# An RWKV, attention, expert and mixer block on one core: group norm beside the gate products, modulation sums in the recurrence

## What is computed

```python
h = rmsnorm(x, norm1_g);  p = h @ w_in
y_a = rwkv7_bidirectional(p_rwkv, ...) @ w_o_rwkv      # ends in a group norm and a gate:
#   y = (y - mean) * rsqrt(var + GN_EPS) * lnx_g + lnx_b     mean and var over each head's 64 channels
#   y = (y + bonus * v) * (sigmoid(gl) @ g_up)
y_b = neighbourhood_attention_2d(q, k, v, ...) @ w_o_na
g_a, g_b = split(sigmoid(gate_logits + b_gate))
x = x + (g_a * y_a + g_b * y_b) @ w_out
x = x + hierarchical_moe(rmsnorm(x, norm2_g), ...)     # 32 experts, 2 per token
# second block: modulation from one row c and one row c_ctx
silu_c @ w_mod + b_mod        # 1024 x 6144, six vectors of 1024
silu_cc @ w_mod + b_mod       # the first two of them for the context
# then the mixer (Hyena, GLA, GatedDeltaNet), the MLP, the final norm
```

## Time and profile before

| | |
|---|---|
| median of 3 runs | 2638.59 us (2636.98 to 2642.66) |
| the profiled execution | 2632.08 us |
| its span | 2630.2 us |
| PE busy | 2106.9 us, 80% |
| DVE busy | 1116.4 us, 42% |
| mean granted clock of TensorE | 0.864 of 2.4 GHz |
| RWKV core | 281 to 706.3 us |
| group norm and gate | 706.3 to 737.0 us |
| output block | 737.0 to 937.8 us |
| modulation, norm | 937.8 to 965.0, 965.0 to 981.8 us |
| router, dispatch | 981.8 to 1010.0, 1010.0 to 1039.0 us |

### The profile page before, as it was taken

How to read it: one execution, slowest core, us unless ns; L and a number is a source line. 1 busy time by engine, 2 the same in 40 slices (tenths; PEclk the granted TensorE clock), 3 DMA queues, 4 the chain that set the end, 5 groups by cost and what they waited for, 6 DMA issues and landing times. The chain is left out here.

```text
span 2630.2 us, 38274 instructions
## 1 busy us (share of the span) xinstructions
PE 2106.9 (80%) x16072; PEld 1599.2 (61%) x16072; DVE 1116.4 (42%) x1705; ACT 642.1 (24%) x1131; POOL 439.3 (17%) x518
## 2 busy tenths in 40 slices
PE   5888589999779964766771999877778875899998
PEld 4666378878667764222220787634677775688886
DVE  6544444344476622000004675232355556432333
ACT  4344222322123210111112453200211112331331
POOL 1000164554101102000001000000234330010100
PEclk9999588888789965898895999978788887999999
DMA  4211000000067401898884112300000002233331
GB/s 177 74 59 49 15 2 2 2 2 2 14 224 267 165 19 42 312 354 313 316 326 146 65 62 72 114 15 20 1 2 2 2 2 74 74 103 96 96 96 56
DMA packets 72449, 252.23 MB, mean 96 GB/s; under 512 B 11462, under 2 KB 12902, under 8 KB 71520
## 3 DMA queue, kind: packets, MB, share of 16 engines
q1 hardware_dynamic: 59584, 213.12, 23.6%
q10 hardware_dynamic: 6912, 25.17, 2.6%
q0 software_dynamic: 5792, 11.62, 1.2%
HBM read 243.84 MB, written 14.69 MB: 98 GB/s over the span
## 5 line engine op out<-in xcount | busy, mean ns | idle before, releaser
L208 PE MATMUL ps<-h_hi,weights_hi 128*128 128x512 f32 x728 | 301.3, 414 | 27.0 <-DVE h_lo L619 7.3
L209 PE MATMUL ps<-h_lo,weights_hi 128*128 128x512 f32 x728 | 291.2, 400 | 0.0
L210 PE MATMUL ps<-h_hi,weights_lo 128*128 128x512 f32 x728 | 290.6, 399 | 0.0
L191 DVE TENSOR_TENSOR weights_lo<-ring,weights_hi 128x1024 fp32r<-128x1024 f32 x162 | 198.9, 1229 | 194.1 <-ACT weights_hi L187 194.1
L187 ACT CAST weights_hi<-ring 128x1024 fp32r<-128x1024 f32 x162 | 169.4, 1047 | 351.5 <-PE ps L210 337.4
L1776 PE MATMUL ps<-ring,sp_rowsT 128*64 128x512 f32 x512 | 143.5, 687 | 81.2 <-DMA ring<-stream_in 80.3
L709 POOL TENSOR_TENSOR gdn_M<-xT,const 64x256 f32<-64x256 f32 x144 | 108.3, 752 | 564.3 <-DVE xT L3036 437.2
L208 PEld LDWEIGHTS ps<-h_hi,weights_hi 128*128 128x128 f32 x728 | 141.1, 194 | 74.3 <-issue 18.4
L210 PEld LDWEIGHTS ps<-h_hi,weights_lo 128*128 128x128 f32 x728 | 141.3, 194 | 30.9
L209 PEld LDWEIGHTS ps<-h_lo,weights_hi 128*128 128x128 f32 x728 | 142.0, 195 | 29.3 <-issue 1.9
L1776 PEld LDWEIGHTS ps<-ring,sp_rowsT 128*64 128x64 f32 x512 | 38.9, 150 | 180.3 <-issue 134.4
(11 more groups left out here) (531 smaller groups left out, 3860.9 us busy)
## 6 DMA issues: line engine op xcount, KB each, us to landing
ring<-stream_in SPq DMA_DIRECT2D x354, 512.0 KB, 4.6
w_mod_ring<-w_mod_in ACTq DMA_DIRECT2D x48, 512.0 KB, 5.2
sp_picks<-picks SPq DMA_DIRECT2D x4, 1024.0 KB, 5.0
na_rel<-rel_in POOLq DMA_DIRECT2D x4, 640.0 KB, 6.1
xT<-xT_in SPq DMA_DIRECT2D x4, 512.0 KB, 5.8
xT<-xT_in SPq DMA_DIRECT2D x1, 2048.0 KB, 9.5
h_tok<-h_by_token SPq DMA_DIRECT2D x4, 512.0 KB
x_mid<-xT SPq DMA_DIRECT2D x1, 2048.0 KB, 7.9
```

The source lines that it names most:

```text
L191: eng.tensor_tensor(self.lo[:, i % self.n, :], self.unit(i)[0], self.hi[:, i % self.n, :], ALU.subtract).then_inc(self.k.used, 1)
L208: pe.matmul(out, left[0], right[0], start=start, stop=False, **kw)
L209: pe.matmul(out, left[0], right[1], start=False, stop=False, **kw)
L210: return pe.matmul(out, left[1], right[0], start=False, stop=stop, **kw)
```

## The change

1. The group norm and gate leave their own stage. Their DVE chain is cut in ten steps, one behind each gate unit's `rest` in the output block; the gate products follow gate unit 0 on PE, the transposes gate unit 10. Gate units now use four PSUM banks, not eight, and weights three buffers, not two. The splits of y and of the mix move from POOL to DVE, and are spread over gate units 11 and 13 and over the `w_o` units.
2. The modulation sums leave the output block for the core: seven behind the levels of each step (1, 2, 1, 1, 2), 64 in all, each with a load of its own (64 where there were 48), through two slots of the stream's ring, into a third slot, from which each of the eight sums is written to DRAM. For this the heads' stream stops three units early.
3. `stage_mod` goes. The eight sums are read back (4096 KB) in the router; 32 of the 64 column sums follow the router's logits on PE, 32 the transposes of the dispatch; `mod` and `gain` are formed at the end of the dispatch's DVE list.
4. The norm before the experts is computed at the end of the output block.
5. h, the mix and Hyena's H share two tiles; others are placed over tiles that are free. These change addresses, not operations.

```diff
+MOD_AT = [[7 * t + (0, 1, 3, 4, 5, 7)[lv] for lv in range(6)] for t in range(10)]
+MOD_AT = [[min(n, (MG + 2) * 8) for n in at] for at in MOD_AT]
...
+                def mod_sum(n):
+                    m, b = divmod(n, DB)
+                    dve.wait_ge(mod_in[n % 2].sem, mod_in[n % 2].at(16 * (n // 2 + 1)))
+                    c = k.silu_c[:, b, m // MG:m // MG + 1]
+                    if b == 0:
+                        if m:
+                            dve.wait_ge(mod_saved.sem, mod_saved.at(16 * m))
+                        dve.tensor_scalar(part, wm[n % 2], c, None, ALU.mult).then_inc(mod_done.sem, mod_done.up())
+                    else:
+                        dve.wait_ge(mod_done.sem, mod_done.at(n))
+                        dve.scalar_tensor_tensor(part, wm[n % 2], c, part, ALU.mult, ALU.add).then_inc(mod_done.sem, mod_done.up())
...
                             if t + 1 < N:
                                 bias(t + 1)
+                        for n in range(MOD_AT[t][lv - 1], MOD_AT[t][lv]):
+                            mod_sum(n)
+
+            @block.sync
+            def _(sp):
+                for n in range((MG + 2) * DB):
+                    m, b = divmod(n, DB)
+                    if n >= 2:
+                        sp.wait_ge(mod_done.sem, mod_done.at(n - 1))
+                    sp.dma_start(wm[n % 2], k.dram["w_mod"][m % MG * DB + b]).then_inc(mod_in[n % 2].sem, mod_in[n % 2].up(16))
+                    if b == 1 and m:
+                        save(sp, m - 1)
...
+                    if i == 0:
+                        pe.wait_ge(got.sem, got.at(48))
+                        for t in range(NT):
+                            mm = pe.matmul(k.ps[:, 4 + t, :], lora[:, 2, t * P:(t + 1) * P], g_up, start=True, stop=True)
+                        mm.then_inc(u_ready.sem, u_ready.up())
+                    if i == 10:
+                        pe.wait_ge(y_done.sem, y_done.at(NT))
...
                 for i in range(16):
-                    w.rest(dve, i + 1)
-                    for u in (2 * i, 2 * i + 1):
-                        mod_sum(dve, mod_seq, u, mod_part[:, u // DB, :], 0)
+                    w.rest(dve, i + 2)
+                    group_norm(i)
...
+                norm.sum(pe)
+                norm.spread(pe)
...
+def mod_sums(k, pe, mod_part, first, last):
+    for m in range(first, last):
+        mm = pe.matmul(k.ps[:, 7, m:m + 1], mod_part[:, m // DB, m % DB * P:(m % DB + 1) * P], k.c("ones")[:, 0:1], start=True, stop=True)
+    return mm
...
+                sp.dma_start(mod_part[:, :, :], k.dram["mod_acc"]).then_inc(part_in.sem, part_in.up(16))
...
+                pe.wait_ge(part_in.sem, part_in.at(16))
+                mod_sums(k, pe, mod_part, 0, 32)
```

More of the change, by code:

```diff
@@ L140, in col, with stream @@
         return self.cols[p0:p1, a + i:a + i + 1]
-    def stream(self, sp, units):
-        end = min(self.taken_at_stage + units + RING, N_UNITS)
+    def stream(self, sp, units, ahead=RING):
+        end = min(self.taken_at_stage + units + ahead, N_UNITS)
         while self.issued < end:
@@ L809, in stage_core @@
         inv = Inverse(k, st, "rw", 0)
+        wm, part = [k.ring[:, (k.issued + i) % RING, :] for i in range(2)], k.ring[:, (k.issued + 2) % RING, :]
+        assert k.issued + 3 == k.taken + RING
         with k.block() as block:
@@ L1370, in stage_merge @@
[L1370 to L1372 removed]
+            rounded, rested, h_scaled = k.sig("rounded"), k.sig("rested"), k.sig("h_scaled")
             @block.tensor
@@ L1418, in _ @@
                 for i in range(16):
-                    w.round(act, i + 1)
-                    load(2 * i)
-                    load(2 * i + 1)
+                    w.round(act, i + 2)
                     w.wait(act, i)
-                    act.activation(g[:, i, :], k.ps[:, i % 8, :], ACT.Sigmoid, bias=k.col("b_gate", i)).then_inc(g_done.sem, g_done.up())
-                for b in range(DB):
-                    act.copy(yab[0][:, b, :], (yaT if b < 4 else ybT)[:, b % 4, :]).then_inc(y_rounded.sem, y_rounded.up())
@@ L1427, in _ @@
-                for i in range(8):
-                    load(32 + 2 * i)
-                    load(33 + 2 * i)
-                    w.round(act, 17 + i)
-                w.wait(act, 23)
-                for i in range(8):
-                    act.wait_ge(m_done.sem, m_done.at(i + 1))
-                    act.copy(mix[0][:, i, :], g[:, i, :]).then_inc(rounded.sem, rounded.up())
-                for i in range(25, 32):
-                    w.round(act, i)
-            def mod_sum(eng, done, u, part, which):
-                eng.wait_ge(mod_in[u % MB].sem, mod_in[u % MB].at(16 * (u // MB + 1)))
-                c = k.silu_c[:, u % DB, which:which + 1]
-                if u % DB == 0:
-                    eng.tensor_scalar(part, wm[:, u % MB, :], c, None, ALU.mult).then_inc(done.sem, done.up())
-                else:
-                    eng.wait_ge(done.sem, done.at(u))
-                    eng.scalar_tensor_tensor(part, wm[:, u % MB, :], c, part, ALU.mult, ALU.add).then_inc(done.sem, done.up())
@@ L1449, in _ @@
-            @block.gpsimd
-            def _(pool):
-                for b in range(DB):
-                    pool.wait_ge(y_rounded.sem, y_rounded.at(b + 1))
-                    pool.tensor_tensor(yab[1][:, b, :], (yaT if b < 4 else ybT)[:, b % 4, :], yab[0][:, b, :],
-                                       ALU.subtract).then_inc(y_rested.sem, y_rested.up())
-                for i in range(8):
-                    pool.wait_ge(rounded.sem, rounded.at(i + 1))
-                    pool.tensor_tensor(mix[1][:, i, :], g[:, i, :], mix[0][:, i, :], ALU.subtract).then_inc(rested.sem, rested.up())
+                    act.activation(g[:, i, :], k.ps[:, i % 4, :], ACT.Sigmoid, bias=k.col("b_gate", i)).then_inc(g_done.sem, g_done.up())
```

380 lines of the change are left out of this document (201 added, 179 removed).

## The result

The changed kernel takes 2657.04 us (median of 5 runs, 2652.9 to 2661.1) against 2636.98 for the kernel before: ratio 1.0079, interval 1.0052 to 1.0105. It is slower by 0.8%, where 2623 was forecast, and outside the range of 2594 to 2656. Its profiled execution took 2654.48 us with a span of 2652.6, so 22.4 more than before.

| stretch | before | after | difference | forecast |
|---|---|---|---|---|
| up to the core | 286.8 | 288.6 | +1.8 | 0 |
| RWKV core | 418.7 | 503.4 | +84.7 | +58 |
| core's end to the router | 276.3 | 198.7 | -77.6 | -77.8 |
| router and dispatch | 58.0 | 63.3 | +5.3 | +4.3 |
| experts to the inverse transform | 732.0 | 728.6 | -3.4 | 0 |

The account below looks back on a forecast made before the run. Serial stretches with little work (group norm, modulation, norm, output block) were to go, while PE paces the core: -73.5 us saved, +58 in the core, -15.5 in sum, so 2623 us, range 2594 to 2656.

Parts of the forecast that it names:

- (a): Group norm's own stage, between core and output block: it goes, saving 30.7 us.
- (b): Output block, norm and modulation: 244.8 us become 197.7, saving 47.1 us.
- (c): Column sums and read-back in router and dispatch: router grows 2.7 us, dispatch 1.6; the 4096 KB read-back costs 0.
- (d): Core, two sums ahead of `scale_state`: PE waits 2.6 us, eight times, 20.5 us.
- (e): Core, one sum ahead of `keep_state`, stretched by POOL's product: 1.1 us late, 9 us for eight (2 to 11).
- (f): Core, two sums behind level 2, delaying `update`: 1.0 us, seven times, 7 us (2 to 17).
- (g): Core, sums at levels 3 and 4 and the first step, where DVE waits for PE anyway: 2.5 us (0 to 6).
- (h): Core, partial sums waiting for their write to DRAM before being begun anew: 11 us (5 to 18).
- (i): Core, PE's slower clock from added idle time: 1 us a step, 8 us; from nothing up to 56.
- the clock turns: Rival: new waits in later core levels bring a second 1.2 GHz stretch each step; up to 2671 us; slower overall: 0.23.
- balance: Rival: a core clock term of 18 to 29 us eats the gain, 2633 to 2644 us; chance 0.15.

Follow-up runs that it names:

- x16: The changed kernel with the two wide tiles back at their old addresses: 2647.9 us, ratio 1.0057 to the kernel before.
- x5: The changed kernel with the two sums ahead of `scale_state` moved right behind it from the third step on: 2621.6 us, ratio 0.9954 to the kernel before.
- x7: x3 with the two sums behind `scale_state` moved ahead of it in six steps: 2597.4 us, ratio 0.9855 to the kernel before.
- x9: The changed kernel with the one sum ahead of `keep_state` moved right behind it from the third step on: 2623.7 us, ratio 0.9971 to the kernel before.
- x14: The changed kernel with two partial-sum buffers and, from the third step on, no sums ahead of `keep_state` or `scale_state`: 2589.3 us, ratio 0.9802.
- x2: The changed kernel with two alternating buffers for the partial sum, one unit less loaded ahead: 2636.6 us, ratio 1.0006 to the kernel before.
- x10: x3 with one sum a step cut in two by columns, its first half ahead of `keep_state`: 2615.7 us, ratio 0.9947 to the kernel before.
- x11: x3 with two sums behind level 2 in place of one, one fewer ahead of the decays: 2581.7 us, ratio 0.9812 to the kernel before.
- x6: x3 with one sum a step moved from behind `keep_state` to ahead of it, seven times: 2620.6 us, ratio 0.9938 to the kernel before.
- x3: The changed kernel with the sums moved into DVE's idle gaps and two partial-sum buffers: 2583.9 us, ratio 0.9795 to the kernel before.
- x1: The changed kernel with the same 64 sums moved into DVE's idle gaps, one partial-sum buffer kept: 2594.9 us, ratio 0.9843 to the kernel before.
- x4: The changed kernel with each sum covering 8 of 1024 columns, loads and writes whole: 2597.9 us, ratio 0.985 to the kernel before.
- x12: x8 with seven sums in most steps and only two steps with a third sum behind `scale_state`: 2574.1 us, ratio 0.9794 to the kernel before.
- x8: x3 with eight sums in most steps, three behind `scale_state`, and few at start and end: 2574.3 us, ratio 0.9777 to the kernel before.

## Why the prediction was wrong, step by step

**(a), (b)**, the stages taken out: right. 77.6 us went between the core's end and the router, of 77.8 forecast, and the block with its norm took 197.6, as forecast 197.7. That is partly luck, since the moved tiles made its 384 gate products dearer (an estimate: 6.9 ns each, from the 8.41 and 8.16 us for 36, so 2.7 us); x16, with the old addresses, has 196.1.

**(c)**: router and dispatch grew by 5.3 and not 4.3. The logits waited 1.6 us longer for their small load, beside which the 4096 KB were being read; the read-back itself came in time, 14.1 us behind its issue. My reason for taking it at nothing was weak: the faster row (`x_mid`, 7.9 us for 2048 KB) is a write to DRAM and not a read.

**(d)**, two sums ahead of `scale_state`: forecast 20.5 us of wait; x5 gave 19.6 back, x7 made 13.5 in six steps. That this wait costs no clock is right by itself (x7), but not in the change, where x5 gave back 9.3 us more: there it lies in a long stretch of 17 to 20 us, where x5 has 14. The second stretch isn't what lengthens it: x9, whose second stretches are gone or 3 to 7 us long, still has 17 to 20, and 8.2 us more busy time than x14, where the waits for `scale_state` are gone too (and the saves, which cost no clock in x2). Why the same wait is free in x7 stays open.

**(e)**, one sum ahead of `keep_state`: the wait was right. PE waited 7.0 us more there (11.2 against 4.2) where I had 9: 1.1 to 1.4 us each, as forecast, but in six steps and not eight, since in the last two POOL's product doesn't meet the sum. In all six the sum took 2.3 us and ended 1.08 us behind POOL's product, and five of x10's half sums ended 0.55 us behind it; the rule of the Trainium skill (SBUF — State Buffer, section SBUF: two separate sides), by which the two operations exclude each other for a whole instruction, agrees with that.

**(f), (g)**: 3.8 us in x11 for 7; the waits ahead of the scores grew from 8.6 to 12.0 us in the change, 3.4 for 2.5. **(h)**, the saves: x2 gave back 10.7 us, for 11.

All waits together: idle time +46.2 us where the steps (d) to (h) had 50.

**(i), the clock, is the step that failed.** I took 8 us, "because the largest new wait, (d), lies within the half-clock stretch, and the others are of a microsecond, as those the row already holds". It was 38.5. The reason was wrong in its second half. PE in one step of the kernel before:

```profile
527.43 1.11 PE L941 MATMUL ps<-rw_Ms,rw_kr 64*128 64x64 f32 x16 [0.52 <-DVE rw_state L1129]
...
537.93 0.66 PE L862 MATMUL ps<-const,rw_bk 128*128 128x128 f32 x4 [1.51 <-DVE rw_bk L1089]
```

The step held a wait of 0.52 us ahead of the outputs, some 7 us behind the clock's rise, and the one of 1.51 us later. The change made the first of them 1.6 to 2.0 in six steps, and that is what opens a second half-clock stretch, of 10 us, in five of them: alone, x6 costs 50 us of half clock, x9 gives back 21.6 us of busy time. So the rival "the clock turns" came true, with its sign and its mechanism. It was priced at up to 7 us a step, and from 3.6 on it decides; in the mean over eight steps it was 4.8, and so the result lies between "balance" and 2671.

The clock is what turned the sign: 30.5 us above its term, against a forecast of 15.5 faster. It alone would have given 2653.5, just inside the range. That the result lies outside is the sum of small things: the waits 3.8 us less, and 11.2 more outside the core, of which 7.1 are the recurrence stage's.

The Trainium skill's rule (TensorE: Matmul & The Clock Gate, section HAM oscillation) holds here only in part: not every late level started slow. The save waits (x2), the waits for `scale_state` (x7) and those behind level 2 (x11) left the clock alone: half clock 274 us without the save waits and 271 with them, PE's busy time 376.5 us in x7 and 377.2 in x3, half clock 152 in x11 and 180 in x3.

**Point 5**, the moved addresses at nothing: wrong. The traces show 5.9 us, 4.4 from the head norm on and 1.5 in the output block; by the medians of x16 and the change it is 9.

The recurrence stage's +7.1 us is not the change's: x2, which differs from the change in the core's buffers alone, has 411.7. Its length lies near one of two values in these profiles: 411.5 to 413.5 in the kernel before, x1, x2, x4, x11 and x12, and 418.5 to 419.3 in the other twelve. The granted clock in it is 0.84 before and in x2, 0.82 in the change and in x8.

## What to carry to other kernels

Work put on an engine that is "half idle" is priced by the place, not by the sum: 64 operations in the gaps in which DVE waited for PE cost 5 us of core (x8, with a second buffer for the partial sum), and the same 64 spread behind the levels with one buffer cost 85. Where PE runs in bursts and the clock has just risen, look at the first long wait behind the rise, and let nothing lengthen it; here a microsecond of it cost two to three more in the slower clock (21.9 us for 12.2 in x6, 21.6 for 7.0 in x9). When tiles are moved, compare the interval between products that read them.

## What the runs showed of the hardware that I had not expected

- In the change, x2, x5, x6, x10 and x16 PE waited 1.45 to 2.9 us ahead of the outputs 36 times, mostly from 6 to 8 us behind the clock's rise. 34 times the clock fell within 3 us of the wait's end, for 10 to 14 us (twice for 7). Both exceptions, 1.78 us in the change and 1.75 in x16, began 5.5 us behind the rise; but three others that began 3.3 to 5.7 us behind it did bring a fall. Waits of up to 2.8 us at the start of the long low stretch cost no clock in x7. How short a wait may be at the first place is open: the waits of 0.5 to 1.0 us there, in all kernels, were followed by such a fall 11 times of 87, each time for 7 us.
- Products of 128x512 that read h from tiles at bytes 65536 and 81920, multiples of 2048, follow each other after 0.2336 us (8.41 us for 36); at 66080 and 82464 after 0.2267 (8.16), 3% less (the change and x16). Which property of the address it is wasn't tried.
- A DVE operation with two tile operands of 512 columns that met POOL's product of 1.77 us ended 0.55 us behind it and took 1.75 us, where alone it takes 0.74 (x10). One of 1024 columns took 2.3 us where alone it takes 1.28, and ended 1.08 us behind (the change).
